# The experts' results are stored through ScalarE's DMA queue in place of GpSimd's

## The reference

```python
xs = h[tok_buf]                              # rows of the tokens, gathered into the experts' blocks
hb = silu(xb @ w_gate[e]) * (xb @ w_up[e])   # xb: the rows of one block, e: its expert
yb = hb @ w_down[e]
out = zeros.at[tok_buf].add(yb * gate)       # each token adds up the results of its two experts
x = layer_norm(alpha * x + (1 + gt2) * out)
```

## Time and profile before

| | us |
|---|---|
| median of 3 runs | 2529.38 (2527.42 to 2529.85) |
| the profiled execution | 2528.53, span 2526.9 |
| TensorE matmul busy | 2212.2 (88% of the span) |
| VectorE busy | 792.7 (31%) |
| ScalarE busy | 449.0 (18%) |
| GpSimd busy | 122.4 (5%) |
| moved by the DMA engines in the whole execution | 395.71 MB, mean 157 GB/s |

### The profile page before, as it was taken

One profiled execution on the slowest core, in us unless ns is written; L12 is line 12 of the kernel. 1 busy time (PEld: TensorE's weight loads), 2 busy tenths in 40 slices (PEclk: granted clock), 3 DMA queues, 4 the chain that ended last, 5 costly groups with the idle time before them and its releaser, 6 DMA issues. The chain is left out here.

```text
span 2526.9 us, 19699 instructions
## 1 busy us (share of the span) xinstructions
PE 2212.2 (88%) x7322; PEld 1074.3 (43%) x7322; DVE 792.7 (31%) x1486; ACT 449.0 (18%) x899; POOL 122.4 (5%) x201
## 2 busy tenths in 40 slices
PE   6988999999999999998999789999996687768673
PEld 2435644434444443544555477444445222222221
DVE  2588411034444102194424745100015010001003
ACT  1122400111111001225324463000002000000001
POOL 0000000000000000000101101000000000000001
PEclk8998899999999999999999889999996899979997
DMA  4226012324444211210110102112340799999996
GB/s 182 95 83 217 34 67 83 125 80 162 157 147 178 75 67 67 100 67 34 67 67 34 67 1 101 67 67 72 132 162 31 298 402 410 411 399 401 404 415 238
DMA packets 41835, 395.71 MB, mean 157 GB/s; under 512 B 6032, under 2 KB 6160, under 8 KB 21648
## 3 DMA queue, kind: packets, MB, share of 16 engines
q1 hardware_dynamic: 23328, 318.43, 32.2%
q0 software_dynamic: 13008, 50.86, 5.8%
q10 hardware_dynamic: 5408, 25.17, 3.0%
HBM read 375.57 MB, written 35.65 MB: 163 GB/s over the span
## 5 line engine op out<-in xcount | busy, mean ns | idle before, releaser
L398 PE MATMUL banks<-arena,ring 128*128 128x512 f32 x1856 | 806.0, 596 | 20.2 <-DVE arena L670 15.3
L1058 PE MATMUL banks<-arena,ring 128*128 128x512 f32 x1424 | 621.1, 597 | 7.6 <-ACT arena L1334 6.0
L398 PEld LDWEIGHTS banks<-arena,ring 128*128 128x128 f32 x1856 | 354.6, 191 | 469.3 <-issue 449.7
L1058 PEld LDWEIGHTS banks<-arena,ring 128*128 128x128 f32 x1424 | 270.4, 191 | 341.2 <-issue 336.7
L2149 PE MATMUL banks<-ring,arena 128*64 128x512 f32 x528 | 134.7, 659 | 60.4 <-DMA ring<-in_experts 42.3
L1329 ACT ACTIVATE arena<-banks 128x512 f32<-128x512 f32 (+5 forms) x151 | 77.5, 520 | 465.7 <-PE banks L1058 328.7
L2149 PE MATMUL banks<-arena 128*64 128x512 f32 x496 | 119.9, 631 | 43.5 <-DMA arena<-in_experts 34.3
L2373 DVE TENSOR_TENSOR arena<-arena,banks 128x256 f32<-128x256 f32 x32 | 13.5, 422 | 395.3 <-ACT arena L2339 395.3
L1155 PE MATMUL banks<-arena 128*128 128x128 f32 x768 | 93.3, 281 | 30.9 <-issue 30.4
L1155 PEld LDWEIGHTS banks<-arena 128*128 128x128 f32 x768 | 90.6, 197 | 33.0 <-issue 31.6
L2149 PEld LDWEIGHTS banks<-ring,arena 128*64 128x64 f32 x528 | 41.6, 150 | 139.5 <-issue 89.3
(11 more groups left out here) (314 smaller groups left out, 1677.5 us busy)
## 6 DMA issues: line engine op xcount, KB each, us to landing
ring<-in_stream SPq DMA_DIRECT2D x53, 2048.0 KB, 8.1
arena<-in_experts SPq DMA_DIRECT2D x52, 2048.0 KB, 31.8
ring<-in_experts SPq DMA_DIRECT2D x44, 2048.0 KB, 31.6
arena<-in_w_adaT POOLq DMA_DIRECT2D x48, 512.0 KB, 4.6
arena<-expert_rows ACTq DMA_DIRECT2D x64, 128.0 KB, 9.2
expert_results<-arena POOLq DMA_DIRECT2D x64, 128.0 KB, 7.5
arena<-in_xT SPq DMA_DIRECT2D x2, 1024.0 KB, 6.3
first_result<-arena POOLq DMA_DIRECT2D x1, 2048.0 KB, 6.6
```

The source lines that it names most:

```text
L398: m = pe.matmul(bank, c.weight(at + k), rhs(k), start=k == 0, stop=k == tiles - 1)
L1058: m = pe.matmul(bank, c.weight(at + k), rhs(k), start=k == 0, stop=k == tiles - 1)
```

## The change

ScalarE gets a function `results(n)` that waits for `output_read` and issues the two stores of expert n. It is called for expert n - 1 at the end of step n, behind `turned(n + 1)`; for expert 15 ahead of the loop over the overflow blocks; and for expert 31 at the end. GpSimd keeps its waits in the middle and at the end, and the stores of the overflow blocks.

```diff
+    def results(n):
+        a.wait_ge(c.sem("output_read"), n + 1)
+        for side in range(2):
+            a.dma_start(slot_rows(c.y_blocks, n)[side],
+                        c.view(YO_ + n % 3 * 512, 512)[side * SLOTS:(side + 1) * SLOTS]) \
+                .then_inc(c.sem(f"stored_rows{n % 3}"), 16)
+
...
     for n in range(NE):
         if n == 0 or n == MID:
             if n:
+                results(n - 1)
                 over_blocks(c, a, body)
             a.wait_ge(c.sem("turned"), n + 1)
             rows(n + 3)
...
             if n + 4 < NE and n + 4 != MID + 2:
                 rows(n + 4)
             turned(n + 1)
+        if n and n != MID:
+            results(n - 1)
+    results(NE - 1)
...
-    for n in range(NE):
-        if n == MID:
-            for j in range(3):
-                g.wait_ge(c.sem(f"stored_rows{j}"), 32 * len(range(j, MID, 3)))
-            g.sem_inc(c.sem("output_free"), 1)
-            g.sem_inc(c.sem("over_free"), 1)
-            over_blocks(c, g, body)
-            g.sem_inc(c.sem("over_done"), 1)
-        g.wait_ge(c.sem("output_read"), n + 1)
-        for side in range(2):
-            g.dma_start(slot_rows(c.y_blocks, n)[side],
-                        c.view(YO_ + n % 3 * 512, 512)[side * SLOTS:(side + 1) * SLOTS]) \
-                .then_inc(c.sem(f"stored_rows{n % 3}"), 16)
+    for j in range(3):
+        g.wait_ge(c.sem(f"stored_rows{j}"), 32 * len(range(j, MID, 3)))
+    g.sem_inc(c.sem("output_free"), 1)
+    g.sem_inc(c.sem("over_free"), 1)
+    over_blocks(c, g, body)
+    g.sem_inc(c.sem("over_done"), 1)
```

## The result

| | before | after |
|---|---|---|
| median, us | 2529.06 (8 runs, 2527.06 to 2529.90) | 2537.53 (8 runs, 2535.70 to 2539.93) |
| ratio, 95% interval | | 1.0036, 1.0025 to 1.0047 |
| span of the profiled execution, us | 2526.9 | 2537.4 |
| last output of VectorE (line 2391, after: 2402), from the span's start | 2490.58 | 2501.51 |
| from there to the end of the span | 36.3 | 35.9 |

The change made the kernel slower by 8.5 us, 0.36%. In the profiled executions all of it arises before the last expert's output, 10.9 us, and the end is 0.4 us shorter.

A forecast was written before the change was run, and what follows sets the result against it. The experts' stage was taken as bound by its bytes on the 16 DMA engines. Packets 1.6, lost company 8.5 and 0 elsewhere gave 10.1 us on 2528.5, 2538.6, with 0.9 for the median predicted as 2539; range 2520 to 2560.

The forecast's parts named there:

- The bound: Experts' stage: lasts as long as its bytes need on the 16 DMA engines; other engines' timing is hidden while queues stay full.
- Step 1, the issue: 64 stores move from GpSimd to ScalarE, hidden in its 7.19 us of idleness: cost 0, without the cover 36 us.
- Step 2, the packets: Stores cut into 2 KB packets like the rows cost 0.05 us more each, 1.6 us over 32; lower bound 0.
- Step 3, the company: On one queue stores follow the rows, no longer between them; lost discount 0 to 14.4 us, 8.5 taken.
- The discount: Rows beside stores cost 1.4 us instead of 2.0 alone: 0.6 us for each of 24 experts.
- Step 4, direction and queue: A store on ScalarE's queue beside the weights still costs 0.61 us for an expert; at most 45 us more in all.
- The rival that priced them as rows: A second hardware queue with 2 KB packets is slow whatever the direction: 2550 to 2575 us, chance 0.16.
- Step 5, the middle: At n = MID over_done comes up to 3.6 us later, hidden by spare time: cost 0.
- Step 6, the end: Last store issued by ScalarE without GpSimd's 0.3 us, before the final gathers: from -0.3 to +0.4 us.
- The signs: Some 400 GB/s, doubled ScalarE packets, stores landing after 10 us or more, longer TensorE weight waits, same tail, over_done before 2248.
- No difference: Rival: the rows' discount comes from a small stretch after the stall and bytes are bytes; 2529 to 2533 us, chance 0.32.
- Faster: Rival: the kernel gets faster by more than 5 us, the rate going above 415 GB/s; chance 0.15.

The follow-up runs named there:

- e11: Repeat of the kernel before with an expert's rows loaded whole by one DMA into 128 partitions, stores on GpSimd's queue: 2507.16 us, 0.9921.
- e12: Repeat of the changed kernel (stores on ScalarE's queue) with rows loaded whole by one DMA into 128 partitions: 2507.34 us, 0.9918 to the kernel before.
- e1: Kernel before, stores still on GpSimd's queue, but mostly held until the rows issued beside them have landed: 2535.90 us, 1.0039.
- e8: Changed kernel with row and store halves issued in turn on ScalarE's queue: 2537.99 us, 1.0038 to the kernel before.
- e10: Kernel before with rows loaded whole into 128 partitions and GpSimd's stores held until the rows have landed: 2506.01 us, 0.9919.
- e4: Kernel before with an expert's rows loaded by one DMA into all 128 partitions instead of two into 64 each: 2507.28 us, 0.9919.
- e9: Kernel before with rows loaded whole into 128 partitions and the experts' result stores left out: 2486.17 us, 0.9838.
- e3: Kernel before without the stores of the experts' results, the results table filled with zeros early: 2516.38 us, 0.9955.
- e2: Changed kernel with queues swapped, GpSimd issuing the rows and ScalarE the stores, at the same time: 2529.74 us, 1.0013 to the kernel before.
- e7: Kernel before with rows in two DMAs, each to every other partition over all 128, stores on GpSimd's queue: 2507.61 us, 0.9919.

## Why the prediction was right

The forecast was 2539 with 2534 to 2549 for its own case; measured 2537.53.

- *The bound.* Right: the loss is in the rate of the DMA engines, and nothing that the other engines did later or sooner is seen in the time. (Of the slices before the experts one, 217 GB/s, is not under half of 400, and the sum with the 0.9 us is 2539.5; neither bears on the forecast.)
- *Step 1, the issue.* Right: 1.22 us for a pair (1.12 assumed), no wait, and ScalarE idle for the same 7.19 us before the silu.
- *Step 2, the packets, 1.6 us.* The packets' own time did rise about as forecast (3.5% of the engines for each MB, 3.4 before), but no loss is seen from it: e11 and e12, which differ in the stores' queue and so in their packets, are 0.2 us apart in the median and 0.1 in the stage. The sum was too high by about this.
- *Step 3, the company, 8.5 us.* Right in that the loss comes when stores and rows no longer travel side by side (e1, e8, e10); in what order the packets go, which the 8.5 us also leaned on, no run shows. The size: the medians moved by 8.5 us and the end gave 0.4 back, so 8.9 us arose before the end, 0.37 for each of 24 experts. The profiled executions alone say 10.9 us. The size is luck: the choice between 0 and 14.4 was made without a row for it, and two terms were off and cancelled.
  The discount itself can be worked out from four kernels. The gain of whole rows over halves is 0.81% with stores (e4) and 1.17% without (e9 against e3), 20.6 and some 30 us; the difference, about 9 us, is what the stores took off (10 us by the stages: 509.0 less 487.1 against 502.3 less 470.2). That is about 0.4 us for each of 24 experts and not 0.6, and the change lost nearly all of it and not a little over half. The intervals are wide (about 6 us either way for the 9), so 14.4 isn't excluded. The price that was too high is the 2.0 us of rows 6 for a row load alone, read from the 25 us right behind the stall in the middle: e3's window gives 1.9, and the 30 us over 28 experts, with 0.61 for the bytes, about 1.7.
- *Step 4, direction and queue.* Right: with stores on ScalarE's queue the stretch without rows still runs at 428 GB/s (e2). The rival that priced them as rows is out. But rows 5 could not price a store: their 428 GB/s counts the stores' own bytes, so the rule gives 0.61 us whatever they cost. e9 measured it, 17.8 us for 32, 0.56 each.
- *Step 5, the middle.* Right: up to 3.6 us later, 3.5 measured, and hidden as said: SP's new loads came 25.1 us after its last one was issued (2208.53 + 16.19 = 2224.72), and that one took 31.0 to land.
- *Step 6, the end.* A little better than the bound of -0.3 us: from VectorE's last output to the first gather 4.47 us, 4.92 before.
- *The signs.* Those on the rate (396), the packets of ScalarE's queue (1461 for 800), the landing of the stores (15.1 us) and the end came. SP's loads came at 2249.81 and not before 2248, because the whole middle came 7.3 us later. "TensorE's waits for weights longer by the loss" did not: 73.9 us, 74.5 before. The loads land later, and TensorE spent the time in slower products.
- *The rivals.* "No difference" failed because bytes are not just bytes here. Its argument that the weights' rate is the same with and without stores misread the rows: 8.44 MB in 25 us is 338 GB/s and 29.98 MB in 80 us is 375; what is the same is their share of the engines' time, 92.2 and 92.0%. "Faster" (0.15) failed too: the kernel is 8.5 us slower. But something real was there to win: an expert's rows and stores, 0.524 MB, would take 1.22 us at 428 GB/s and cost 2.0, so 0.78 us were lost, 19 us for 24 experts, of which the lower end of the range, 2520, takes half. e4 wins 20.6 us, and the change of queue nothing.

What I called company is shown as a dependence on time (e1, 1.0039) and on two queues (e8, 1.0038). Why a store beside rows helps, and why the weights' packets take longer without it (92.4% of the engines for 29.23 MB, before 92.0% for 29.98), no run shows.

## What to carry to other kernels

Try to write SBUF over all 128 partitions, also with small DMAs. Here an expert's rows in two DMAs of 64 partitions, one half each, cost the saturated load stream 1.4 to 2.0 us where their bytes would take 0.61, two to three times as much. Written by one DMA over all 128, rows and stores together cost 2.5 us for each MB, where bytes alone take 2.3 (e4), and rows by two DMAs to every other partition left the same 427 GB/s (e7). When the DMA engines set the pace, price a small transfer by what the big stream loses in its presence, in windows with and without it, and not by its own packets' time; and before moving it, look at what travels at the same time. If a gap stays between the price and the bytes, look for its cause before moving transfers around it: here the move cost 0.36% and the cause gave 0.8%.

## What the runs showed of the hardware that I had not expected

- Taking 8.4 MB of stores out of a saturated stage gave 8.3 us with rows in halves and about 18 with whole rows, 3 us at the end not counted in either: the price of one stream depends on how another writes.
- Two small streams in two queues, issued at the same time, cost less together (2.0 us for an expert from 2120 to 2200 us) than the same two in one queue (2.6 us), with the same bytes and nearly the same packet time. Issued at different times they lost this also in two queues (1.0039). The order of the DMAs within the one queue made no difference that can be seen (1.0036 and 1.0038).
- A DMA to every other partition, with a step in the leading dimension of the SBUF side, left room for as much beside it as one to 128 partitions in a row (427 GB/s in all, both times).
